# Keeping half of the output weights on chip: four fixed places, and a ring of 15 instead of 19

## What is computed

```python
m = sigmoid(g_conv) * conv_out + sigmoid(g_attn) * attn_out
h = layer_norm(ALPHA * x + einsum('ntd,de->nte', m, w_out), ln1_g, ln1_b)   # w_out: 1024 x 1024
...
# 8 heads x 16 experts = 128 slots per token, picked by two top-16 searches over product keys
u = peer_u[eidx]                       # one row of 1024 for each token and slot
v = peer_v[eidx]
a = gelu(einsum('nd,nhed->nhe', x2, u))
out = einsum('nhe,nhed->nd', g * a, v)
```

## Time and profile before

| | |
|---|---|
| median of 3 runs | 2060.43 us (2060.42 to 2067.68) |
| the profiled execution | 2049.36 us, its span 2047.4 us |
| DVE busy | 1288.3 us (63%) |
| PE busy | 1264.5 us (62%) |
| POOL busy | 1172.7 us (57%) |
| moved by DMA | 699.49 MB, mean 342 GB/s |
| fetches through the ring | 544 u, 544 v, 32 parts of `w_out` |

### The profile page before, as it was taken

How to read it: one execution, slowest core, us unless ns; L and a number is a source line. 1 busy time by engine, 2 the same in 40 slices (tenths; PEclk the granted TensorE clock), 3 DMA queues, 4 the chain that set the end, 5 groups by cost and what they waited for, 6 DMA issues and landing times.

```text
span 2047.4 us, 19306 instructions
## 1 busy us (share of the span) xinstructions
PE 1264.5 (62%) x6055; PEld 556.7 (27%) x6055; DVE 1288.3 (63%) x3102; ACT 338.0 (17%) x900; POOL 1172.7 (57%) x1143
## 2 busy tenths in 40 slices
PE   8997998886741766665367596752322244765425
PEld 4563443452410224332021252410100011221101
DVE  5329979971266867947668499375498996013341
ACT  1510020221100541200044221100100001100000
POOL 1005446735565566656666566566476677446675
PEclk9998998988875885687688657876566556888768
DMA  8819989978999899999999999999799959999997
GB/s 335 339 60 392 338 312 366 333 251 308 339 363 358 329 351 360 402 345 357 356 406 379 337 350 394 339 374 370 243 387 342 403 213 396 361 364 381 372 364 298
DMA packets 213504, 699.49 MB, mean 342 GB/s; under 512 B 27573, under 2 KB 55733, under 8 KB 206579
## 3 DMA queue, kind: packets, MB, share of 16 engines
q0 software_dynamic: 162560, 598.44, 77.7%
q1 hardware_dynamic: 43691, 90.66, 12.3%
q10 hardware_dynamic: 7152, 9.17, 1.2%
HBM read 685.66 MB, written 12.94 MB: 341 GB/s over the span
## 4 chain that ended last, share of the span: by engine, by line
DVE 32%; PE 25%; issue 18%; DMA 7%; POOL 6%; another core or an unknown queue 5%; ACT 3%; SPq 3%; DVEq 0%; ACTq 0%; POOLq 0%
DVE rings L2464 14%; PE acc L2008 6%; POOL rings L1010 6%; DMA rings<-peer_v,late 3%; PE bank L1698 3%; PE bank L1724 3%; PE bank L1573 2%; DVE small L2074 2%; DVE uah L2077 2%; PE acc L1490 2%; DVE zt L2274 2%; DMA conv_acc<-causal 1%; DVE conv_acc L2274 1%; DMA w_conv_out_s<-cache_kT 1%
## 5 line engine op out<-in xcount | busy, mean ns | idle before, releaser
L1010 POOL DMA_INDIRECT rings<-peer_u,late x544 | 608.6, 1119 | 417.6 <-DVE late L2464 154.1
L1010 POOL DMA_INDIRECT rings<-peer_v,late x544 | 530.9, 976 | 327.3 <-issue 137.3
L2008 PE MATMUL acc<-rings,z_stages 128*32 128x512 f32 x2048 | 364.9, 767 | 390.5 <-DMA rings<-peer_v,late 162.3
L2464 DVE CUSTOM_DVE_ANT_0 rings<-rings,wide 128x1024 f32<-128x1024 f32 x256 | 299.7, 1216 | 27.6 <-DMA rings<-peer_u,late 15.6
L2008 PEld LDWEIGHTS acc<-rings,z_stages 128*32 128x32 f32 x2048 | 86.1, 130 | 640.3 <-issue 637.3
L2464 DVE CUSTOM_DVE_ANT_0 rings<-rings,uah 128x1024 f32<-128x1024 f32 x160 | 191.6, 1222 | 86.8 <-DMA rings<-peer_u,late 72.8
L2464 DVE CUSTOM_DVE_ANT_0 rings<-rings,late 128x1024 f32<-128x1024 f32 x128 | 153.7, 1221 | 8.4 <-DMA rings<-peer_u,late 6.9
L1523 PE MATMUL acc<-rings 128*128 128x512 f32 (+1 forms) x352 | 155.6, 591 | 4.2 <-DMA rings<-w_in 3.4
L1424 ACT COPY z_stages<-late 128x4 f32<-128x4 f32 x136 | 25.4, 197 | 433.6 <-remote 232.9
L1854 PE MATMUL bank<-keep,soft_score 128*128 128x64 f32 x288 | 63.5, 389 | 49.6 <-ACT soft_score L1235 27.9
L1523 PEld LDWEIGHTS acc<-rings 128*128 128x128 f32 x352 | 66.4, 203 | 77.6 <-issue 73.3
(11 more groups left out here) (316 smaller groups left out, 1705.1 us busy)
## 6 DMA issues: line engine op xcount, KB each, us to landing
rings<-w_in SPq DMA_DIRECT2D x35, 1024.0 KB, 8.7
rings<-w_out POOLq DMA_DIRECT2D x32, 512.0 KB
rings<-peer_u,late POOLq DMA_INDIRECT x544
rings<-peer_v,late POOLq DMA_INDIRECT x544
z_rows<-z_stages ACTq DMA_DIRECT2D x30, 256.0 KB
soft_score<-ln SPq DMA_DIRECT2D x6, 1024.0 KB
zt<-z_rows SPq DMA_DIRECT2D x2, 2596.0 KB
rings<-w_out POOLq DMA_DIRECT2D x4, 1024.0 KB, 7.6
```

The lines of the kernel that those rows point to most:

```text
L1010: nc.gpsimd.indirect_dma_start(ring[:, place, :], None, table, offs).then_inc(row_in[place], 16)
L2008: last = nc.tensor.matmul(acc_v[QUAD * j:QUAD * (j + 1), half * BLK:(half + 1) * BLK], lone[:, quad % LONE, j, QUAD - 1 - m:2 * QUAD - 1 - m],
L2464: V.tensor_tensor_reduce(out=ring[:, place, :], in0=ring[:, place, :], in1=h, scale=1.0, scalar=0.0, op0=ALU.mult, op1=ALU.add, accum_out= ...
```

## The change

Row chunks 0 to 3 of `w_out` (`OUT_KEPT` = 4) stay in places 11 to 14 for the whole kernel, where tile 0's copy lies already. `homes()` gives these four places to nobody, so the ring has 15 places, and 12 once the v fetches of tile 3 begin. `out_loaded(t)` are the parts that are still loaded per later tile: 2, 3, 6 and 7 for tiles 1 to 3, and 4 to 7 for the samples. The other 16 of the 32 parts are not fetched. The products read chunks 0 to 3 from the fixed places, and the count of the semaphore `out_used`, by which POOL knows that a part has been used, is made to fit. The number and the order of all other instructions stay.

```diff
-PLACES, W_PLACES, OUT_PLACES, OUT_AT = 19, 6, 8, 11
+PLACES, W_PLACES, OUT_PLACES, OUT_AT, OUT_KEPT = 19, 6, 8, 11, 4
...
+    def out_loaded(t):
+
+        return [k for k in range(OUT_PLACES) if out_part(t, k)[0].start >= OUT_KEPT]
+
+    def out_given_back(t):
+
+        return [k for k in out_loaded(t) if not out_ends(t, k)]
+
     def out_uses(t, k):
 
-        return (t - 1) * (OUT_PLACES - 2) + sum(not out_ends(t, j) for j in range(k + 1))
+        return sum(len(out_given_back(j)) for j in range(1, t)) + out_given_back(t).index(k) + 1
...
-        weights = [(out_needed(t, k) - OUT_LEAD, ("w", t, k)) for t in range(1, N_TILES + 1) for k in range(OUT_PLACES)]
+        weights = [(out_needed(t, k) - OUT_LEAD, ("w", t, k)) for t in range(1, N_TILES + 1) for k in out_loaded(t)]
...
-            place = min(range(n_places), key=lambda p: free[p])
+            in_turn = [p for p in range(n_places) if not OUT_AT <= p < OUT_AT + OUT_KEPT]
+            place = min(in_turn, key=lambda p: free[p])
...
-                if t == 0:
+                if t == 0 or c < OUT_KEPT:
                     weights = wou[:, c, half * BLK:(half + 1) * BLK]
...
-                if t and c % 2 and c < KC - 1:
+                if t and c >= OUT_KEPT and c % 2 and c < KC - 1:
                     last.then_inc(out_used, 1)
...
-                place, landed, _ = HOMES["w", S_T, c]
-                pe.wait_ge(row_in[place], landed)
+                if c >= OUT_KEPT:
+                    place, landed, _ = HOMES["w", S_T, c]
+                    pe.wait_ge(row_in[place], landed)
+                else:
+                    place = OUT_AT + c
...
-                last.then_inc(out_used if c < KC - 1 else out_mm, 1)
+                if c >= OUT_KEPT:
+                    last.then_inc(out_used if c < KC - 1 else out_mm, 1)
```

## The result

The changed kernel takes 2040.54 us (median of 9 runs, 2032.27 to 2051.81), the kernel before 2060.56 us (9 runs, 2049.67 to 2067.68). The ratio is 0.9906, interval 0.9879 to 0.9933: 0.9% faster, some 19 us. The forecast of 2065 us had the sign wrong, and its range (2043 to 2086) ended just above the result.

What follows compares the result with a forecast made beforehand. No engine bounds it by its sum; DMA and consumers alternate, with the ring as stock between them. Terms 0 - 5 + 2 + 3 + 0 + 3 + 1.6 = +4.6 us gave 2054 us profiled, 2065 us as median; range 2043 to 2086 us.

Steps and rivals of the forecast that it cites:

- What the change removes: Sixteen unfetched w_out parts: tiles 1 to 3's twelve worth 0 (other bound 14.9 us gain), the samples' four -5 us.
- the samples' four: Samples' parts near late v rows at 1784 and 1803 us: each delays a row by a transfer, -5 us.
- step 4: 1746 to 1763 us: with 12 places, rows 16 to 19 of tile 3 not on chip; +3 us, bounds 0 and 5.3.
- Step 1: Tile 1's dots, about 735 to 751 us: rows late, mostly covered by DVE's later standstill; +2 us, 0 to 10.7.
- Step 2: Tile 3's dots, about 1457 us: shorter burst, four more rows awaited, search hands delay on; +3 us, bounds 0 and 4.6.
- Step 3: About 1657 to 1680 us: dots up to 4.4 us late, covered by the wait for keys; 0, bound +4.4 us.
- Step 5: From 1855 us: up to four rows missing after the routing's pause, mostly hidden by queued transfers; +1.6 us, bounds 0 and 5.
- the 11.1 us: Whole kernel: runs' median 2060.43 us above the profiled execution, turning the forecast of 2054 us into 2065 us.
- Bandwidth: Rival, whole stream: DMA limits, each removed part counts wherever it stood, 20 to 22 us faster, 2040 us; chance 0.13.
- Stock paid in full: Rival, stalls at 741, 903, 1433, 1746 us: missing stock never regained, +25 us, 2085 us; chance 0.28.
- Consumers setting the pace: Rival, everywhere it matters: stock and traffic both hidden, no change, 2060 us; chance 0.11.

Runs made afterwards that it cites:

- d19_thin_parts: Kernel before, all 32 parts keeping turn, place and issue, but the 16 the change drops move 256 bytes a partition instead of 4096: ratio 0.9982.
- after_again: The changed kernel measured once more, for a second profile: 2045.97 us, ratio 0.9917 to the kernel before.
- d19_unissued: Kernel before, ring of 19, with the change's 16 parts not transferred but keeping turn, wait and place: ratio 0.9954.
- after_lead15: The changed kernel with its 16 parts issued a nominal 15 us ahead of their product instead of 30: ratio 0.9881 to the kernel before.
- before_lead15: Kernel before with parts issued a nominal 15 us ahead of their product instead of 30: ratio 1.0029.
- depth19_half: The changed kernel with its ring back at 19, 16 parts loaded, each used for both halves of the sum: 2046.08 us, ratio 0.989 to before.
- before_lead60: Kernel before with parts issued a nominal 60 us ahead of their product instead of 30: ratio 1.0028.
- d19_spare_issues: Kernel before, ring of 19, 16 parts without turn or place, a tiny transfer outside the ring issued at each one's position: ratio 0.9878.
- depth15_all: Kernel before with its ring cut to 15 places, all 32 parts still loaded through it: ratio 1.0069.
- kept8_ring11: The change driven on: eight chunks kept for tiles 1 to 3, five for the samples, 3 parts loaded, ring of 11: ratio 0.9884 to before.
- d19_no_parts: Kernel before, ring of 19, no part loaded for any later tile, products reading the query weights instead: ratio 0.991.
- d19_samples_halved: Kernel before, ring of 19, only parts 0 to 3 of the samples left out: ratio 0.9924.
- d19_tiles_halved: Kernel before, ring of 19, only the twelve parts 0, 1, 4, 5 of tiles 1 to 3 left out: ratio 0.9927.
- fixed_places: Ring of 11 as in kept8_ring11, but all 32 parts transferred, 29 into fixed places outside the ring: ratio 1.0006 to the kernel before.
- both kernels with a pause: Kernel before with POOL waiting for ACT's copies of tile 1's h before row 16 or row 24 of tile 0: ratios 1.0054 and 0.9991.

## Why the prediction was wrong

**Where the gain lies.** The spans between events, in us, worked out from the traces by the starts of instructions: A, DVE's dot 96 of tile 0 to PE's sum 16 of tile 0 (about tile 1's product); B, first matmul of tile 2's product to sum 16 of tile 1; C, first sum of tile 3 to its sum 64 (about the samples' attention and product).

```
turns kept                A      B      C     fewer turns            A      B      C
before                131.1   64.4  125.6     after              129.4   60.6  112.8
d19_thin_parts        135.7   59.5  118.7     after_again        124.2   61.1  113.8
d19_unissued          136.4   66.4  118.4     after_lead15       126.5   58.6  111.7
before_lead15         142.7   57.2  109.9     depth19_half       135.7   56.6  112.2
before_lead60         134.2   66.4  119.9     d19_spare_issues   126.6   61.1  107.6
depth15_all           131.4   67.8  135.5     kept8_ring11       125.4   62.1  116.2
                                              d19_no_parts       124.9   58.1  107.2
d19_samples_halved    131.0   66.3      -     d19_samples_halved     -      -  103.3
d19_tiles_halved          -      -  108.4     d19_tiles_halved   127.4   58.2      -
```

The two halved kernels stand in either half by what they keep in the stretch. The means with eight turns are 134.6, 64.0 and 119.5 us, with four or none 127.5, 59.6 and 110.6. The differences, 7.1, 4.5 and 8.9, make 20 us, the size of the gain, though single traces cross over, in C above all. fixed_places has 123.5, 60.2 and 121.5: without turns A and B are short even with all bytes moved, C is not; nor is the whole faster (1.0006).

A goes with ACT's standstill described above: 9.3 to 19.9 us, 15.7 in the mean, with eight turns, 1.1 to 16.3, 6.8 in the mean, with four or none. And this goes with POOL's run of row fetches after the product: 24 in a row, with less than 1 us of idle time between them, in six of the seven traces with eight turns (13 in depth15_all), 12 to 20 in the others. That is a chain read from traces: fewer parts, fewer places that come free at once, a shorter run, a shorter standstill. Yet both kernels with a pause have a short A too (125.8 and 120.9 us) and win nothing at the end, their B (65.1 in both) and C (121.8 and 111.9) being as with eight turns. So how much of the 20 us comes from A is not shown.

About tile 3's product nothing is gained (first matmul to sum 16 of tile 2, 65.1 us in before, 68.5 in after).

**What the change removes: the step that failed.** "I take 0" for the twelve parts of tiles 1 to 3, with 14.9 us as the other bound, and -5 us for the samples' four. Measured alone they are worth 15 and 16 us, together 23 (11 to 34). The twelve were thus at their bound. Its reason, that POOL is held up by places there anyway, priced a part as an issue that disappears in a wait. Even the row that it rests on did not bear that out: 13 waits, 13.9 us in all, for the 24 parts of tiles 1 to 3, so 11 of them waited for no dot.

But a part isn't only an issue: it takes a place that would have gone to a row at its turn. The runs show 13 to 21 us between sixteen parts that keep the turn without their bytes and sixteen that are gone (thin and unissued parts against spare issues and left-out ones, each difference uncertain by 13 to 15), and, across two groups, 0.9 us for each transfer and issue where the turn is gone. Either alone gone wins little or nothing. The counting "with eight parts in 19 places 11 are left for rows, with four in 15 also 11" was right, and missed that the rows go from 19 to 11 and back in one case and from 15 to 11 in the other; that this swing is what costs is argued, not shown.

The samples' four were sized by the delay of single transfers. The two late v rows shrank by 5.15 us together, as forecast; but from sum 4 to sum 64 of tile 3 a ring of 19 takes 105.0, 98.3, 97.9 and 102.5 us with eight turns (before, thin, unissued, d19_tiles_halved) and 91.8, 95.6, 95.5 and 91.7 with four or none, some 7 us less in all, and the keys' wait comes on top (step 4). In the change itself, with its ring of 15, this stretch is hardly shorter (103.3, 101.1 and 99.8 us in after, after_again and after_lead15); there C is shorter than in before mostly by the keys' wait.

**Step 1.** Place and lateness were right, and the cover held; the +2 us didn't come. The dot that ran at 741.28 us in before waits 3.00 us for its row and runs 3.8 us later (4 had been forecast). Behind it DVE stands still for something else, 7.84 and 11.24 us before (the second is in the earlier trace rows), 10.70 and 5.99 us after, and the score step that stood at 785.69 us comes at 784.04:

```profile
745.11 1.22 DVE L2477 CUSTOM_DVE_ANT_0 rings<-rings,wide 128x1024 f32<-128x1024 f32 x1 [3.00 <-DMA rings<-peer_u,late]
...
764.36 0.56 DVE L2304 CUSTOM_DVE_ANT_0 soft_score<-bank,soft_score 128x384 f32<-128x384 f32 x1 [10.70 <-remote]
...
775.66 0.56 DVE L2304 CUSTOM_DVE_ANT_0 soft_score<-bank,soft_score 128x384 f32<-128x384 f32 x1 [5.99 <-remote]
...
784.04 0.56 DVE L2304 CUSTOM_DVE_ANT_0 soft_score<-bank,soft_score 128x384 f32<-128x384 f32 x1
```

**Step 2.** The burst is as forecast, the cost is not: a burst of 7 dots instead of 11, and POOL's long issue 5.53 us where 9.41 stood, about 5 having been expected. Four dots less (4 x 1.15 us) shorten it by 3.9: by the Trainium skill's rule (SBUF — State Buffer, "Who interferes with whom") the trace agrees, and in both traces the issue ends 0.8 us after the burst. The other kernels bear it out: POOL's longest issue there is 9.1 to 9.8 us in the eleven other traces with a ring of 19, 7.25 us with 17, 4.6 to 5.5 us with 15, and at most 2.4 us with 11.

```profile
1461.10 5.53 POOL L1019 DMA_INDIRECT rings<-peer_u,late  x1 [25.78 <-PE acc L2021]
```

```profile
1471.92 1.23 DVE L2477 CUSTOM_DVE_ANT_0 rings<-rings,uah 128x1024 f32<-128x1024 f32 x1 [6.11 <-DMA rings<-peer_u,late]
```

The twelfth dot counted from the start of the burst comes 3.0 us later than in before (21.9 us against 18.9), the size forecast. But the search did not hand it on: the dots stay 5.8 us behind those of before up to about 1540 us, where DVE of before stands still for something else, and from about 1562 us they are 1.7 us ahead. From before:

```profile
1549.84 0.69 DVE L2084 BATCH_NORM_STATS2 small<-bank 32x6 f32<-32x512 f32 x1 [7.30 <-remote]
```

**Step 3.** Its rows come 4.5 us late at dots 104 to 120 of tile 3 (from the dots' starts in both traces), the bound of 4.4, and the keys' wait covers it. **Step 4.** Wrong in sign in these two traces: the keys land in 8.98 us instead of 18.62, and row 16 of tile 3 starts 9.9 us earlier than before (1766.9 against 1776.9 us), not 3 us later. The text had named this ("fewer rows go ahead of the keys") and valued it below the missing stock. This wait varies, however: 5.9 to 20.5 us from the first sum of tile 3 to its fifth in twelve traces with a ring of 19, five of them at 20.4 or 20.5; 7.2 to 12.7 us in six with 15 or 11. So the long case was not met with a short ring, but that the fewer rows are the cause is not shown. **Step 5** is not told apart: sum 64 of tile 3 to the first of the samples takes 149.7 and 148.9 us in the traces of the change, 140.7 in that of before, and 144 to 159 in the other traces with a ring of 19.

**The sum.** The steps come to +4.6 us against the profiled execution, and the profiled after is +1.7 us from it. That the two are near each other is luck: steps 1 and 2 were swallowed, step 4 had the other sign (sum 64 of tile 3 starts at 1854.4 us instead of 1866.0), and behind it 9 us are lost again. The execution before was also a fast one of its kernel: of 133 later runs of it ten are faster. I added the 11.1 us to its median as if any kernel lost them in a typical run. The seven later traces with a ring of 19 and eight turns before tiles 1 to 3 have spans of 2052.7 to 2081.5 us, that of before has 2047.4: what the change wins was hardly in the trace that the steps were read from.

**The rivals.** Bandwidth gave 2040 us, the number measured, and its mechanism does not hold by itself: thin parts move 7.9 MB less and win 0.2% (-0.1 to 0.5). Bytes have a share in it, as fixed_places suggests, but only together with the turn. The rule beside it (the Trainium skill, DMA: Bandwidth & Descriptors, "Where 436 GB/s comes from"), by which a mean of 342 GB/s is nearly full, would have made them win as much as the change; the trace doesn't agree, as after runs at 395 GB/s from 1675 to 1725 us. Stock paid in full falls: POOL's waits did not grow, and the four places cost nothing that can be measured once the parts are gone (to within 14 us). Consumers setting the pace falls with the result.

**What stays open.** Why a part costs what it does. Sixteen parts without their bytes win 4 us (uncertain by 6), without bytes and issue 9 us (by 7), gone altogether about 20; half the holding time wins nothing, and the four places cost nothing measured once the parts are gone. What remains is the shape of the flow: rows stop coming for eight turns, then eight places come free at once. About tile 1's product the traces show this shape as a run of 24 row fetches and a standstill of ACT; that it is the cause of the whole gain is argued, not shown. Nor do I know why parts beyond sixteen bring nothing, or whether two kept chunks bring anything.

## What to carry to other kernels

A load that shares a ring with a stream can't be priced by its bytes or its issue alone; take them away one at a time, with a thin transfer that keeps the turn, a tiny one that has none, and the whole transfer into a place of its own, and expect that neither alone gives the gain. A queue that is often blocked by places is no proof that an entry less is free: count how many of these very entries waited, and how long. Before summing steps against a profiled execution, see where it stands among its kernel's runs: at the fast end, part of what a typical run loses isn't in it, and a change can win what the trace doesn't show.

## What the runs showed of the hardware

A run of 24 row fetches, one every 1.24 us, held up work that shares nothing with it by the program: ACT's copy stood 14.20 us with its input ready, 1.85 us when POOL paused after five fetches and 5.22 us when it paused after thirteen. Over the seventeen traces without a pause the standstill goes with the length of the run (14.2 to 19.9 us in five of the six with 24 fetches, 12.8 in the sixth; 1.1 and 3.2 us with 12). The DMA engines were full meanwhile (500 to 520 us of before, the first row; 490 to 504 us of the kernel with the pause, the second):

```profile
500.00:520.00 20.00, 5.65 (x38) 2.74 (x30) 0.00 (x0) 1.37 (x4) 13.41 (x15) 0.62 1.02 410
```

```profile
490.00:504.00 14.00, 11.02 (x55) 4.04 (x53) 4.64 (x9) 2.39 (x5) 4.05 (x5) 1.00 0.56 189
```

What ACT waited for is not in the traces: no transfer other than rows is recorded from 489 to 526 us of before.

And the spread of one kernel is 1 to 2% from run to run (2043.74 to 2075.57 us over 23 runs of before in one group), with the same program and data; a difference of half a per cent needed twelve runs of a kernel against some thirty of the other, and even then left 7 us of uncertainty.
